# Issuing DRAM copies and centred-row stores from ScalarE, with one more weight slot and a shorter closing stage, in a one-core decoder layer

## What is computed

```python
z = jnp.einsum("bsd,de->bse", h, w_in) + b_in
glu_val, glu_gate, gate_c, q, k, v, f_logit, gate_a = _split_columns(z)
y_conv = _conformer_conv(glu_val, glu_gate, w_dw, b_dw, g_cn, b_cn)
y_conv = y_conv * jax.nn.silu(gate_c)
y_attn = _forgetting_attention(q, k, v, f_logit)
y_attn = y_attn * jax.nn.silu(gate_a)
y = jnp.concatenate([y_conv, y_attn], axis=-1)
sub = jnp.einsum("bse,ed->bsd", y, w_out) + b_out
h = _layer_norm(DN_ALPHA * h + sub, g_post, b_post)
```

## Time and profile before

| what | value |
|---|---|
| median of 3 runs | 1633.11 us (1632.91 to 1633.67) |
| the profiled execution | 1634.14 us |
| its span, first to last instruction | 1632.4 us |
| PE busy | 1566.7 us (96%) |
| DVE busy | 1442.6 us (88%) |
| ACT busy | 838.4 us (51%) |
| POOL busy | 274.8 us (17%) |
| moved by DMA | 367.33 MB, 225 GB/s |
| mean granted TensorE clock | 0.989 of full |

### The profile page before, as it was taken

How to read it: one execution, slowest core, us unless ns; L and a number is a source line. 1 busy time by engine, 2 the same in 40 slices (tenths; PEclk the granted TensorE clock), 3 DMA queues, 4 the chain that set the end, 5 groups by cost and what they waited for, 6 DMA issues and landing times.

```text
span 1632.4 us, 29443 instructions
## 1 busy us (share of the span) xinstructions
PE 1566.7 (96%) x11574; PEld 1492.5 (91%) x11574; DVE 1442.6 (88%) x1952; ACT 838.4 (51%) x1224; POOL 274.8 (17%) x295
## 2 busy tenths in 40 slices
PE   7999999999999999999999999999977999999995
PEld 7999999999999999999999999998977877778884
DVE  7669999999999999999999999999865679886885
ACT  4465454554554545545455455454443566644461
POOL 1011212122122121221212212201222100010000
PEclk9999999999999999999999999999989999999998
DMA  8488988999999999999999999998988998687673
GB/s 224 102 193 190 223 206 202 241 225 234 222 215 231 233 223 235 207 249 225 210 233 237 226 216 220 243 227 190 245 207 207 317 321 321 205 282 220 230 230 137
DMA packets 316761, 367.33 MB, mean 225 GB/s; under 512 B 14593, under 2 KB 254369, under 8 KB 315313
## 3 DMA queue, kind: packets, MB, share of 16 engines
q1 hardware_dynamic: 287184, 264.65, 52.7%
q0 software_dynamic: 27360, 100.68, 34.1%
q10 hardware_dynamic: 2080, 0.13, 0.1%
HBM read 286.73 MB, written 87.06 MB: 229 GB/s over the span
## 4 chain that ended last, share of the span: by engine, by line
PE 70%; DVE 13%; DMA 7%; issue 6%; ACT 3%; POOL 0%; SPq 0%; DVEq 0%; ACTq 0%; POOLq 0%
PE ps L1043 23%; PE ps L1044 23%; PE ps L1045 23%; DVE whl L1284 3%; DMA conv_rows_dram<-cin 2%; DVE c_tiles L1385 2%; DVE whl L1287 2%; ACT whl L748 1%; PE ps L1156 1%; DMA raw<-raw 1%; DVE yl L1537 1%; DMA raw<-out_sums_dram 1%; DMA raw<-in_w_in_dram 1%; ACT aff_c L992 1%; DVE yc L1598 1%
## 5 line engine op out<-in xcount | busy, mean ns | idle before, releaser
L1043 PE MATMUL ps<-xh,whl 128*128 128x256 f32 x3136 | 897.1, 286 | 35.5 <-ACT nu L845 23.5
L1044 PE MATMUL ps<-xl,whl 128*128 128x256 f32 x3136 | 889.7, 284 | 0.0
L1045 PE MATMUL ps<-xh,whl 128*128 128x256 f32 x3136 | 889.7, 284 | 0.0
L772 ACT ACTIVATE whl<-raw 128x1024 fp32r<-128x1024 f32 x392 | 415.3, 1061 | 594.1 <-PE ps L1045 467.5
L1043 PEld LDWEIGHTS ps<-xh,whl 128*128 128x128 f32 x3136 | 601.9, 192 | 39.8 <-ACT nu L845 24.1
L1044 PEld LDWEIGHTS ps<-xl,whl 128*128 128x128 f32 x3136 | 602.3, 192 | 0.3 <-issue 0.2
L1045 PEld LDWEIGHTS ps<-xh,whl 128*128 128x128 f32 x3136 | 601.9, 192 | 0.0
L1284 DVE TENSOR_TENSOR whl<-raw,whl 128x1024 fp32r<-128x1024 f32 x392 | 481.8, 1229 | 83.8 <-ACT whl L772 83.5
L1385 DVE SCALAR_TENSOR_TENSOR c_tiles<-ps,taps,c_tiles 128x511 f32<-128x511 f32 (+14 forms) x480 | 350.0, 729 | 6.9
L1287 DVE TENSOR_TENSOR whl<-raw,whl 128x1024 fp32r<-128x1024 f32 x106 | 129.5, 1221 | 57.7 <-ACT whl L748 57.7
L1043 PE MATMUL ps<-whl,yh 128*128 128x512 f32 x424 | 167.9, 396 | 10.4 <-DVE yl L1537 7.3
(11 more groups left out here) (177 smaller groups left out, 1313.7 us busy)
## 6 DMA issues: line engine op xcount, KB each, us to landing
raw<-in_w_in_dram SPq DMA_DIRECT2D x224, 512.0 KB, 7.8
raw<-raw POOLq DMA_DIRECT2D x112, 512.0 KB, 5.8
out_sums_dram<-in_w_out_dram POOLq DMA_DIRECT2D x64, 512.0 KB, 9.5
raw<-out_sums_dram SPq DMA_DIRECT2D x64, 512.0 KB, 5.0
raw<-in_w_out_dram SPq DMA_DIRECT2D x48, 512.0 KB, 4.7
out_sums_dram<-in_w_out_dram SPq DMA_DIRECT2D x32, 512.0 KB, 9.5
out_sums_dram<-out_sums_dram SPq DMA_DIRECT2D x32, 512.0 KB, 9.6
x<-in_x_dram SPq DMA_DIRECT2D x8, 512.0 KB, 8.1
```

The source lines that it names most:

```text
L772: nc.scalar.activation(w_high(n), source(n), ACT.Copy).then_inc(high_done, 1)
L1043: nc.tensor.matmul(o, ah, bh, start=start, stop=False, skip_group_check=True)
L1044: nc.tensor.matmul(o, ah, bl, start=False, stop=False, skip_group_check=True)
L1045: return nc.tensor.matmul(o, al, bh, start=False, stop=True, skip_group_check=True)
```

## The change

Five things are edited.

1. The DRAM-to-DRAM copies (`copies`) leave SP and are issued by ACT at the end (slot 6) of a group. T1 and T3 (and T2 of an earlier head) go out in a group with `g % 3 == 2`, T4 with `g % 3 == 0`.
2. The store of centred row `j` leaves SP: ACT issues it in `square(j)`, ahead of the squaring. SP's `load_cin` keeps its waits.
3. At the start: `f_terms` of the last factor stands ahead of the last transposes, `forget` is earlier on ACT and DVE, and the last transposed bank goes to R5 (`x_bank`), so that unit (1, 1) waits for 24 of 28 banks only.
4. In the second product: a fourth weight slot (`whl_more`), weights prepared three units ahead (`AHEAD`), a denser `NORM_AT`, with `finish_conv` at +2 and `gated` at +3, and the read-out of product 7 two units earlier.
5. At the end: `END` is 6, not 8; both banks of n = 0 are done unit by unit; then (1, 0) and (1, 1) as before.

```diff
-NORM_AT = (4, 6, 8, 10, 12, 14, 17, 20, 23, 26, 29, 32, 34, 36, 38, 40)
-END = 8
+NORM_AT = (4, 6, 8, 10, 12, 14, 16, 19, 22, 24, 27, 30, 32, 34, 36, 38)
+END = 6
 E0 = OUT_UNITS - END
+
+FOUR = 5
+AHEAD = 3
...
         def x_bank(j):
-            return (BANK_A, BANK_B, BANK_C, R1_ODD)[j % 4]
+            return R5 if j == X_BANKS - 1 else (BANK_A, BANK_B, BANK_C, R1_ODD)[j % 4]
...
-            q = u - E0
-            if q < 0:
+            if u >= E0:
+                return w_end[u - E0][:, low, :]
+            if u < FOUR:
                 return whl[:, out_n(u) % SLOTS, low, :]
-            if q < 6:
-                return w_end[q][:, low, :]
-            return whl[:, (UNITS + E0 + q - 6) % SLOTS, low, :]
+            slot = (3, 1, 2, 0)[(u - FOUR) % 4]
+            return whl_more[:, low, :] if slot == 3 else whl[:, slot, low, :]
...
-            def store_cent(j):
-                sp.wait_ge(cent_done, j + 1)
-                sp.dma_start(conv_dram[j, :, :], cin[:, j % 4, :]).then_inc(cent_stored[j % 4], 16)
-
             def load_cin(j):
                 if j >= 4:
-                    store_cent(j - 4)
                     sp.wait_ge(sq_done, j - 3)
                     sp.wait_ge(cent_stored[j % 4], 16 * (j // 4))
...
                 loads(g)
-                copies(g)
...
+            def copy_sum(t, k, src, copied):
+                nc.scalar.dma_start(t_dram[t, k, :, :], src).then_inc(copied, 16)
+
+            def copies(g):
+
+                k = g // 3 - 1
+                if g % 3 == 2 and 0 <= k < HEADS:
+                    act.wait_ge(t_added[T1], 16 * (k + 1))
+                    if k:
+                        act.wait_ge(t2_copied, 16 * k)
+                    copy_sum(T2, k, t_dram[T1, k, :, :], t2_copied)
+                k = g // 3 - 3
+                if g % 3 == 0 and 0 <= k < HEADS:
+                    act.wait_ge(t_added[T2], 16 * (k + 1))
+                    if k:
+                        act.wait_ge(t4_copied, 16 * k)
+                    copy_sum(T4, k, t_dram[T2, k, :, :], t4_copied)
+                k = g // 3
+                if g % 3 == 2 and k < HEADS:
+                    if k:
+                        act.wait_ge(t13_copied, 32 * k)
+                    copy_sum(T1, k, w_out[D + P * k:D + P * (k + 1), 0:1024], t13_copied)
+                    copy_sum(T3, k, w_out[D + P * k:D + P * (k + 1), 1024:], t13_copied)
...
                 act.wait_ge(cent_done, j + 1)
                 if j >= 2:
                     act.wait_ge(sq_added, j - 1)
+                nc.scalar.dma_start(conv_dram[j, :, :], cin[:, j % 4, :]).then_inc(cent_stored[j % 4], 16)
                 nc.scalar.activation(c_tiles[:, j % 2, :], cin[:, j % 4, :], ACT.Square).then_inc(sq_done, 1)
...
             for u in range(1, E0):
-                high(out_n(u + 2))
+                if u <= 2:
+                    high(out_n(u + 2))
+                if u >= 2:
+                    high(out_n(u + AHEAD))
...
                 for j in range(HEADS):
-                    if u == NORM_AT[j] + 1:
+                    if u == NORM_AT[j] + 2:
                         finish_conv(j)
...
-                if g == 1 and m == 1:
+                if g == 1 and m in (1, 5):
+                    pe.wait_ge(xl_done, X_BANKS if m == 5 else X_BANKS - 4)
+                if (g, m) == (0, 4):
                     pe.wait_ge(xl_done, X_BANKS)
...
-            for n in range(2):
+            for u in range(E0, OUT_UNITS):
+                ready(u)
                 for g in range(2):
-                    for u in range(E0, OUT_UNITS):
-                        if n == 0 and g == 0:
-                            ready(u)
-                        last = out_mm(u, n, g)
-                    last.then_inc(end_done, 1)
+                    last = out_mm(u, 0, g)
+                    if u == OUT_UNITS - 1:
+                        last.then_inc(end_done, 1)
+            for g in range(2):
+                for u in range(E0, OUT_UNITS):
+                    last = out_mm(u, 1, g)
+                last.then_inc(end_done, 1)
...
-                    if g == 1 and s in (0, 2):
-                        forget(s)
+                    if (g, s) == (1, 1):
+                        forget(1)
...
                     if g == 0 and s == 6:
+                        forget(0)
                         x_low(2)
...
-                if u in (44, 45, 46, 47):
-                    n, g = divmod(u - 44, 2)
+                if u in (42, 43, 44, 45):
+                    n, g = divmod(u - 42, 2)
```

More of the change, by code:

```diff
@@ L207, in build @@
         over.close()
+        sb("parts_b", [P, 2048], F32, over)
+        whl_more = sb("whl_more", [P, 2, 1024], F32R, over)
+        over.close()
         sb("parts_a", [P, 2 * PT_LEN], F32, over)
@@ L220, in build @@
         yl = sb("yl", [P, 2, SEQ], F32R, over)
-        yh_end = sb("yh_end", [P, 2, SEQ], F32R, over)
-        yl_end = sb("yl_end", [P, 2, SEQ], F32R, over)
         over.close()
@@ L233, in build @@
         nu1 = sb("nu1", [P, TOK])
+        yh_end = sb("yh_end", [P, SEQ], F32R, over)
+        yl_end = sb("yl_end", [P, SEQ], F32R, over)
+        over.close()
         c_tiles = sb("c_tiles", [P, 2, SEQ])
@@ L322, in y_pair @@
         def y_pair(ring_y, end, v):
-            last = v - E0 // 2
-            return end[:, last, :] if 0 <= last < 2 else ring_y[:, v % 2, :]
+            return end[:, :] if v == E0 // 2 else ring_y[:, v % 2, :]
         def out_bank(m, n, g):
@@ L531, in _ @@
                         load_cin(j)
-            for j in range(HEADS - 4, HEADS):
-                store_cent(j)
             def load_a(half, q):
@@ L938, in _ @@
                         x_high(4)
-                    if (g, s) in ((0, 6), (1, 1)):
-                        forget(g)
+                    if (g, s) == (0, 6):
+                        forget(0)
                     evict(g, s)
@@ L947, in _ @@
                     gates(g, s)
+                    if s == 6:
+                        copies(g)
                     if g == 0 and s == 6:
@@ L1031, in _ @@
                     scale_rows(2 if u == 93 else 3)
-            for u in range(E0 + 2, OUT_UNITS):
-                high(out_n(u))
-                if u % 2 == 0:
-                    y_high(u // 2)
+            for v in range(E0 // 2 + 1, OUT_PAIRS):
+                y_high(v)
+                if E0 + AHEAD <= 2 * v:
+                    high(out_n(2 * v))
+                high(out_n(2 * v + 1))
             deviation(2)
@@ L1196, in _ @@
                     if g == 0 and s == 5:
+                        f_terms(((3, 5, 1),)).then_inc(f_done, 1)
+                        for b in range(3):
+                            turn_x(2, b)
                         pe.wait_ge(dw_loaded, 16)
@@ L1725, in _ @@
             for u in range(1, E0):
-                low(out_n(u + 2))
+                if u <= 2:
+                    low(out_n(u + 2))
+                if u >= 2:
+                    low(out_n(u + AHEAD))
                 if u % 2 == 0:
@@ L1741, in _ @@
                 early_rows(u)
-            for u in range(E0 + 2, OUT_UNITS):
-                low(out_n(u))
-                if u % 2 == 0:
-                    y_low(u // 2)
+            for v in range(E0 // 2 + 1, OUT_PAIRS):
+                y_low(v)
+                if E0 + AHEAD <= 2 * v:
+                    low(out_n(2 * v))
+                low(out_n(2 * v + 1))
             dve.wait_ge(bout_added, 32 * NT)
```

52 lines of the change are left out of this document (17 added, 35 removed).

## The result

The changed kernel takes **1617.14 us** in the median of 4 runs (1616.06 to 1622.57), the kernel before in the same session 1633.39 us (1632.91 to 1635.77). The ratio is **0.9904, with a 95% interval of 0.988 to 0.9928**: faster by 16 us, where I had forecast 35 us. The time lies above my range (1584 to 1612). Run again later, beside 15 runs of the kernel before, it had 0.9924 (0.9887 to 0.9962). The profiled execution of after took 1622.57 us, the slowest of the four, at a span of 1620.8 us; that of before 1634.14 and 1632.4 us. One execution further down (e5, 3904.9 us) was a slow one and is left out; e5's times are those of its other three.

A forecast was written before the change was run, and what follows sets the result against it. PE was taken to bound 200 to 1100 us, so gains lay outside: -18 (late groups), -6 (start), -6 (second product), -6.5 (end), +1 (copies) make -35.5 us. Likeliest time 1598 us, range 1584 to 1612 us.

The forecast's parts named there:

- Centred rows: End of first product: stores issued by ACT let SP load weights earlier; three late groups gain 18 us.
- Copies on ACT: First product: issuing the copies on ACT delays its high part slightly, mostly absorbed by spare time; charged 1 us.
- the rival with the largest issues: First product: at the largest issue durations PE loses 24 us, giving 1621 us, or 1606 at a third; chance 0.08.
- No charge: Waits that come along with the copies on ACT are for transfers mostly a group or more back; no cost.
- Start: 80 to 100 us: earlier forget gate work and the last bank in R5 gain 6 us, between 3 and 7.
- Second product: Fourth weight slot, longer lead and wider-spaced steps win back 6 of 8.3 us, between 2 and 8.
- Closing stage: End: six matmuls between waits, not three, return 8.0 of 8.6 us; net 6.5, between 4 and 7.
- the tail: After the last matmuls: DVE needs 9.4 us for additions against PE's 7.9, so it begins 1.5 us late.
- ACT held by the copies: First product: long copy issues on ACT delay PE; 1621 us at the largest durations, 1606 at a third; chance 0.08.
- The 16 engines bind: Late groups: DMA share stays at 0.94, so they take 82.0 us and give 6.6; 1609 us; chance 0.14.
- no limit: Late groups: DMA engines set no limit, groups run at 19.8 us each; 1586 to 1587 us; chance 0.17.
- The rival that ends slower than before: First product: copy issues from 2.3 us each on ACT eat all gains; 1641 us at 2.4 each; chance 0.03.

The follow-up runs named there:

- e5: Kernel before with only the stores of centred rows moved to ACT; 1620.47 us, ratio 0.9898.
- e11: Kernel before with only the stores of centred rows moved to ACT, run again for its trace; 1621.61 us, ratio 0.9909.
- e7: Changed kernel with copies back on SP and POOL's accumulating additions to T2 and T4 cut to 128 of 1024 columns from group 50 on; 1611.22 us, ratio 0.9807.
- e12: Changed kernel, all copies still on ACT, with the T4 copy at slot 3 and gate rows loaded three units later; 1603.38 us, ratio 0.98.
- e1: Changed kernel with the DRAM copies back on SP at their old place; 1613.18 us, ratio 0.9861.
- e6: Changed kernel with the copies back on SP and gate rows loaded three units later; 1606.02 us, ratio 0.978.
- e4: Changed kernel with SP's load of gate rows three units later; 1616.6 us, ratio 0.9844.
- e2: Changed kernel with only the T4 copy moved from slot 6 to slot 3, still on ACT; 1616.33 us, ratio 0.9868.
- e8: Changed kernel, copies on SP, later gate rows, but the old NORM_AT, finish_conv and gated steps and product 7 read-out; 1617.3 us, ratio 0.9849.
- e3: Kernel before with only the copies moved to ACT at slot 6; 1645.91 us, ratio 1.0061.
- e9: Kernel before, unchanged, run again for a second trace; 1638.13 us, ratio 1.0001.
- e10: Changed kernel, unchanged, run again for a second trace; 1626.11 us, ratio 0.9924.

## Why the prediction was wrong, point by point

- **Centred rows: right, size within 2 us.** Forecast -18, with 68 to 74 us for the three groups; measured 72.7 us, -15.9, and e11 shows that the edit does it alone. That the load on the DMA engines now holds part of it, e7 shows. The figures inside that term were not right, though: I reached 72 us with 77.1 us of work at a share of 1.07, and the row of after has 0.96 x 72.7 = 69.8 us of work at a share of 0.96. The busy time of before was no fixed amount of work, and the share did not rise above 1 over so long a stretch. Part of the work had moved out of the window, as I had guessed: 261 x 72.7 = 19.0 MB against 228 x 88.6 = 20.2 MB in before. The two errors cancelled, which was luck.
- **Copies on ACT: the step that failed.** I charged 1 us, and measured +11.9 us in the profiled execution, of which 87 x 0.121 = 10.5 us lie between 200 and 1100 us. I priced the *issue* on ACT from SP's medians, with ACT's idle time and DVE's spare time as cover, and the rival with the largest issues gave 24 us by the same reasoning. The issues are in fact cheaper on ACT (0.61 and 0.48 us), and e12 has them all on ACT with no matmul lost. In the medians the loss is smaller, 7 us (e1 against after) and 10 us (e6 against e4). What I wrote of the waits ("No charge") passed over the sentence that followed from it: the change moves not only who issues, but *when* the transfer runs. The T4 copy starts 6.8 us later in its group, beside loads that have little margin. Putting that one copy back by three slots returned 7406 (e2) against 7332, and 7419 (e12) against 7307 (e4). The rule of the Trainium skill that I weighed, in DMA: Bandwidth & Descriptors, section "Issuing engines are not separate DMA queues", says that transfers share the same 16 engines and interleave whoever issued them. The ratios of e12 and e6 agree with it as closely as can be measured here (0.98 and 0.978). I used it for the late groups alone; held against the copies, it would have led me to ask what they share the engines with once they start later.
- **Start: right in mechanism, smaller.** `neg_cum` came 5.1 us earlier, at 63.37 us against 68.45, as forecast. It gave 3.6 us, not 6: 80 to 100 us has 133 matmuls and not 165, and PE still waits 2.7 us, where it had waited 3.5, for the eviction that I had counted as covered. The bound of 3 to 7 held it.
- **Second product: the second step that failed, wrong sign.** Forecast -6, measured +2.8; the two stretches of 40 us have 166 and 156 matmuls and not 170. I wrote that SP "is held one unit longer at each gate row load, which takes a unit from the lead of the weights behind it", and still took 6 of 8.3 us. That wait has twelve occurrences, 66.9 us, against 49.4 us in before; ACT's idle time for weights from `out_sums_dram` is 27.8 us, against 8.6 in before. The term needed a lower bound below zero. e4 takes the hold away and wins 10.0 us, e8 shows that table, steps and read-out win 7.5 us by then. That part of the mechanism in my sum existed, behind a wait that ate it; for the other part, the fourth slot with its lead, no run shows a gain.
- **Closing stage: right, somewhat larger.** Forecast 8.0 us back, measured 8.9 (97 matmuls in 21.9 us, not 30.8), part of it clock: the mean granted clock of that stretch was 0.89 of full in before and 1.00 in after. For the tail I had said 1.5 us late; it was 0.4. The net gain of 8.5 us is above my bound of 7. DVE adds the last rows right when PE is done:

```profile
1608.41 0.39 PE L1050 MATMUL ps<-w_end,yh 128*128 128x512 f32 x1
1608.64 0.39 PE L1051 MATMUL ps<-w_end,yl 128*128 128x512 f32 x1
```
```profile
1606.53 2.48 DVE L1785 SCALAR_TENSOR_TENSOR res<-res,rs,bpost_b 128x1024 f32<-128x1024 f32 x2
1608.93 1.27 DVE L1638 TENSOR_TENSOR res<-res,ps 128x512 f32<-128x512 f32 x2
```

The forecast sum was -35.5, the measured one -11.6 in the profiled execution and about -16 in the median. The difference of the two in the traces is 23.9 us: 10.9 in the steady stretch, 8.8 in the second product, 2.4 at the start, 2.1 in the late groups, 1.7 in the marks around them, and 2.0 less at the end. With both mends (e12) the kernel is 33.8 us below the 1637.21 us of its session. That is near what I had forecast for the change itself, so the two terms that failed are what the forecast missed by.

Of the rivals, the one with a time near the measured one, ACT held by the copies (1606 to 1621), is wrong in what it says: no issue is long, and ACT waits for weights. "The 16 engines bind" asked for 82 us in the three groups and has 72.7; "no limit" asked for 59.3. The rival that ends slower than before is true of the copies alone (e3), by another mechanism than the one I gave it.

**What stays open.** Up to group 49 several of these kernels are the same program, and their counts of matmuls in the steady stretch show how much one execution differs from the next:

| same program in the stretch | matmuls |
|---|---|
| kernel before (before, e9, e11) | 7419, 7419, 7400 |
| kernel before, copies on ACT at slot 6 (e3) | 7388 |
| changed, copies on SP (e1, e6, e7, e8) | 7419, 7399, 7357, 7382 |
| changed, T4 copy at slot 6 (after, e10, e4) | 7332, 7346, 7307 |
| changed, T4 copy at slot 3 (e2, e12) | 7406, 7419 |

In the changed kernel the loss is 73 to 112 matmuls with the T4 copy at slot 6, and 0 to 62 without, so the copy's moment costs something on top. But weights also land late at times with the copies on SP. What makes an execution lose there, and how much of the 87 matmuls of after was that, is not settled.

## What to carry to other kernels

Price a moved DMA by when it will run and what it will then meet, not by the issue on its new engine. For every wait that a table of unit numbers moves earlier, look at what is queued behind the waiting instruction; a wait for landing or for data on the queue that also loads weights was worth 10 to 16 us here, each time. And where PE shows no wait at all in a stretch, its weights may still land with little to spare: count its matmuls first in the trace after.

## What the runs showed of the hardware

The same DRAM-to-DRAM copies took 0.61 and 0.48 us to issue from ACT and 0.92 and 0.91 us from SP. From ACT the issues of plain copies also landed sooner; medians from 200 to 1100 us, after and then e1:

```profile
out_sums_dram<-in_w_out_dram ACTq DMA_DIRECT2D x28, 512.0 KB, 6.7
out_sums_dram<-out_sums_dram ACTq DMA_DIRECT2D x27, 512.0 KB, 6.3
```
```profile
out_sums_dram<-in_w_out_dram SPq DMA_DIRECT2D x28, 512.0 KB, 9.6
out_sums_dram<-out_sums_dram SPq DMA_DIRECT2D x27, 512.0 KB, 9.7
```

Whether that comes from the queue or from the moment, these rows don't tell. An issue on ACT also stands in the trace at 253.31 us while the step that began at 253.29 us (1.06 us long) still ran, so it did not wait for ACT's work to end. The issue of one weight load on SP (ns min/median/max, in e1) took 0.57 us in the median and 9.7 us at most:

```profile
L399 SPq DMA_DIRECT2D raw<-in_w_in_dram x224: 367/574/9722, 3.0 to 1242.7; - x112
```

So a median says little of what a single issue can cost the queue behind it.
